# Expert biases by VectorE shuffles, and gathered rows in 1 KB pieces turned by VectorE, in a hybrid block with 32 experts

## The reference

```python
logits = u2 @ router_w + router_b
top_val, top_idx = lax.top_k(logits, 4)
gates = softmax(top_val)
# for each expert e, on the tokens that chose it:
hcat = xb @ w1[e] + b1[e]                  # 1024 -> 2048
h_glu, h_lin = split(hcat)
act = min(h_glu, 7) * sigmoid(1.702 * h_glu) * (clip(h_lin, -7, 7) + 1)
y = act @ w2[e] + b2[e]                    # 1024 -> 1024
# out = rms_norm(h + sum over the four of gate * y)
```

## Time and profile before

| | |
|---|---|
| median of three runs | 1619.48 us |
| span of the profiled execution | 1597.8 us |
| PE busy | 1571.5 us, 98% |
| VectorE (DVE) busy | 649.7 us, 41% |
| ScalarE (ACT) busy | 384.0 us, 24% |
| POOL busy | 444.7 us, 28% |
| moved by DMA | 493.10 MB, 309 GB/s over the span |

### The profile page before, as it was taken

One profiled execution on the slowest core, in us unless ns is written; L12 is line 12 of the kernel. 1 busy time (PEld: TensorE's weight loads), 2 busy tenths in 40 slices (PEclk: granted clock), 3 DMA queues, 4 the chain that ended last, 5 costly groups with the idle time before them and its releaser, 6 DMA issues.

```text
span 1597.8 us, 38945 instructions
## 1 busy us (share of the span) xinstructions
PE 1571.5 (98%) x16458; PEld 902.0 (56%) x16458; DVE 649.7 (41%) x1249; ACT 384.0 (24%) x601; POOL 444.7 (28%) x513
## 2 busy tenths in 40 slices
PE   7999999999999999999999999999999999999997
PEld 6998988877889644334433344334433443344334
DVE  4799898016242742224222332233222322232248
ACT  5333134346222311111111121122112111211112
POOL 7334333462433642111211111111211121112114
PEclk9999999999999999999999999999999999999999
DMA  7553242321275699999999999999999999999995
GB/s 217 159 179 112 79 144 95 90 72 51 79 294 224 204 340 406 407 416 414 412 398 410 412 409 398 414 407 408 394 411 407 410 392 404 411 412 400 403 413 236
DMA packets 129781, 493.10 MB, mean 309 GB/s; under 512 B 14379, under 2 KB 72099, under 8 KB 79973
## 3 DMA queue, kind: packets, MB, share of 16 engines
q1 hardware_dynamic: 110932, 464.61, 74.6%
q0 software_dynamic: 9168, 16.78, 3.2%
q10 hardware_dynamic: 9632, 11.03, 2.2%
HBM read 476.32 MB, written 24.87 MB: 314 GB/s over the span
## 4 chain that ended last, share of the span: by engine, by line
PE 95%; POOL 1%; ACT 1%; SPq 1%; DMA 1%; DVE 1%; issue 0%; POOLq 0%; DVEq 0%; ACTq 0%
PE banks L1619 41%; PE banks L1147 27%; PE banks L1668 21%; PE banks L1606 2%; DMA stage<-in_w_in_dram 1%; PE banks L1551 0%; PE banks L1639 0%; SPq L461 0%; PE banks L1506 0%; POOL h_res L787 0%; PE banks L1379 0%; POOL w_lo L624 0%; POOL w_lo L633 0%; POOL small L611 0%; SPq L447 0%
## 5 line engine op out<-in xcount | busy, mean ns | idle before, releaser
L1619 PE MATMUL banks<-w_ring,xT 128*32 128x512 f32 x6144 | 670.9, 592 | 0.1
L1619 PEld LDWEIGHTS banks<-w_ring,xT 128*32 128x32 f32 x6144 | 197.8, 110 | 431.3 <-issue 422.4
L1668 PE MATMUL banks<-w_ring,actT 128*32 128x256 f32 x6144 | 343.9, 380 | 0.0
L1668 PEld LDWEIGHTS banks<-w_ring,actT 128*32 128x32 f32 x6144 | 195.3, 110 | 144.8 <-issue 19.3
L2118 DVE TENSOR_TENSOR hid<-banks,bias 128x512 f32<-128x512 f32 x96 | 63.8, 665 | 475.6 <-PE banks L1619 475.6
L633 POOL TENSOR_TENSOR w_lo<-stage,w_hi 128x2048 fp32r<-128x2048 f32 x38 | 175.3, 4614 | 258.0 <-ACT w_hi L832 258.0
L1147 PE MATMUL banks<-u_hi,w_hi 128*128 128x264 f32 (+1 forms) x528 | 176.8, 335 | 1.5 <-POOL w_lo L624 1.5
L1147 PE MATMUL banks<-u_hi,w_lo 128*128 128x264 f32 (+1 forms) x528 | 175.1, 332 | 0.0
L1147 PE MATMUL banks<-u_lo,w_hi 128*128 128x264 f32 (+1 forms) x528 | 174.7, 331 | 0.0
L706 POOL COPY token_now<-token_of 96x1 int32 x32 | 6.6, 205 | 541.0 <-PE banks L1606 540.9
L1108 ACT ACTIVATE bias<-banks 128x512 f32<-128x512 f32 x32 | 19.1, 598 | 568.4 <-PE banks L1639 568.4
(11 more groups left out here) (311 smaller groups left out, 1586.7 us busy)
## 6 DMA issues: line engine op xcount, KB each, us to landing
w_ring<-in_expert_w_dram SPq DMA_DIRECT2D x384, 1024.0 KB, 17.6
stage<-in_w_in_dram SPq DMA_DIRECT2D x20, 1024.0 KB, 5.3
stage<-in_w_in_dram SPq DMA_DIRECT2D x16, 512.0 KB, 5.6
y_rows<-empty_row ACTq DMA_DIRECT2D x8, 1024.0 KB, 4.8
y_in<-y_rows SPq DMA_DIRECT2D x4, 2048.0 KB, 20.8
stage<-in_conv_pw_w_dram SPq DMA_DIRECT2D x4, 1024.0 KB, 5.2
stage<-in_mlstm_out_w_dram SPq DMA_DIRECT2D x4, 1024.0 KB, 5.2
stage<-in_w_out_dram SPq DMA_DIRECT2D x4, 1024.0 KB, 5.5
```

Source lines behind the costliest of these rows:

```text
L1619: last = nc.tensor.matmul(banks[32 * g:32 * (g + 1), t].rearrange("p (c j) -> p c j", j=64), xT[:, k, 32 * t:32 * (t + 1)], units, start=k ...
L1668: last = nc.tensor.matmul(banks[32 * g:32 * (g + 1), 3 + t, 0:GRP], actT[:, t, k], w2_ring[k // 2][:, k % 2, GRP * g:GRP * (g + 1)], start ...
```

## The change

Two parts.

*Biases.* They are loaded once in a layout in which partition 32g + e has the biases of expert e for the columns of group g (bias_turn, 128x768 float32, eight DMAs). For each expert a VectorE shuffle copies partition 0 of each block of 32 to all 32 (bias1, 512 columns; bias2, 256 columns), and another turns bias_turn by one partition in each block. The products on TensorE, the copies and the row pick on ScalarE, and the split on VectorE are gone.

*Rows.* u2 is written with its columns regrouped, so that a token's row in DRAM is four pieces of 1 KB. A gather is now three indirect DMAs (one for each group of 32 slots) of 128 pieces: piece g of a slot's token goes to partition 32g + slot. Slots are dealt over the 32 partitions of a block in steps of four (SPREAD = 8, TURNS = 4): slot s of a group stands in partition 4 * (s % 8) + s // 8. VectorE transposes the pieces in 32x32 blocks into xT. The slot tables are read back by 16 loads and converted on POOL in three rounds. w_router is loaded in eight DMAs, and last_g on POOL's queue.

```diff
-            sp.dma_start(w_router, router_w[0].rearrange("(k p) e -> p k e", p=P)).then_inc(router_in, 16)
+            for h in range(2):
+                for k in range(CG):
+                    sp.dma_start(w_router[32 * k:32 * (k + 1), h::2],
+                                 router_w[0].rearrange("(h k g j) e -> h k j g e", h=2, k=CG, g=CG)[h, k]).then_inc(router_in, 16)
...
-            sp.dma_start(last_g, final_norm_g.rearrange("(a d) -> a d", a=1).to_broadcast([P, D])).then_inc(row_bc_in, 16)
...
-                pool.indirect_dma_start(out=xs, out_offset=None, in_=u2_dram,
-                                        in_offset=bass.IndirectOffsetOnAxis(ap=token_now, axis=0),
-                                        bounds_check=last_token, oob_is_err=False).then_inc(xs_in, 16)
+                for t in range(TG):
+                    pool.indirect_dma_start(out=xs[:, t], out_offset=None, in_=u2_pieces,
+                                            in_offset=bass.IndirectOffsetOnAxis(ap=piece_now[:, t:t + 1], axis=0),
+                                            bounds_check=last_piece, oob_is_err=False).then_inc(xs_in, 16)
...
-            pool.dma_start(token_of[:, 0:PASSES * NE].rearrange("i (q e) -> i q e", e=NE),
-                           by_slot).then_inc(table_in, 16)
+            by_turn = table.rearrange("(x b a e) o -> b a x (e o)", b=TURNS, a=SPREAD, e=NE)
             for g in range(CG):
-                for t in range(TG):
-                    pool.dma_start(row_of[32 * g:32 * (g + 1), t, 0:PASSES * NE].rearrange("i (q e) -> i q e", e=NE),
-                                   by_slot[32 * t:32 * (t + 1)]).then_inc(rows_in, 16)
-            pool.wait_ge(table_in, 16)
-            chain(nc.gpsimd.tensor_scalar(token_part, token_of, -1.5, 0.25, ALU.add, ALU.mult))
-            chain(nc.gpsimd.tensor_scalar(token_part, token_part, TO_WHOLE, None, ALU.add))
-            chain(nc.gpsimd.tensor_scalar(token_of, token_part, -TO_WHOLE, None, ALU.add))
+                for b in range(TURNS):
+                    pool.dma_start(code_of[32 * g + b:32 * (g + 1):TURNS], by_turn[b]).then_inc(rows_in, 16)
+            pool.wait_ge(rows_in, 16 * CG * TURNS)
+            for t in range(TG):
+                codes = code_of[:, t::TG]
+                pieces = piece_of[:, t, 0:PASSES * NE].rearrange("p (q e) -> p q e", e=NE)
+                rows = row_of[:, t, 0:PASSES * NE].rearrange("p (q e) -> p q e", e=NE)
+                chain(nc.gpsimd.tensor_scalar(token_part, codes, -1.5, 0.25, ALU.add, ALU.mult))
+                chain(nc.gpsimd.tensor_scalar(token_part, token_part, TO_WHOLE, None, ALU.add))
+                chain(nc.gpsimd.tensor_scalar(token_part, token_part, -TO_WHOLE, None, ALU.add))
+                nc.gpsimd.tensor_scalar(pieces, token_part, float(CG), group_of, ALU.mult, ALU.add)
+                chain(nc.gpsimd.tensor_scalar(rows, codes, float(CG), group_of, ALU.mult, ALU.add))
+            pool.dma_start(last_g, final_norm_g.rearrange("(a d) -> a d", a=1).to_broadcast([P, D])).then_inc(last_g_in, 16)
...
-                    pool.wait_ge(xs_used, n + 2)
+                    pool.wait_ge(xT_made, (n + 2) * TG)
                     gather(n + 2, n * IDX + 4)
...
-                    act.wait_ge(bias_mm, n * 2 + 1)
-                    nc.scalar.activation(bias1, banks[:, 3].rearrange("p (h n) -> p h n", h=2), ACT.Copy).then_inc(bias_made, 1)
-                    act.wait_ge(bias_mm, n * 2 + 2)
-                    nc.scalar.activation(bias2, banks[:, 4, 0:GRP], ACT.Copy).then_inc(bias_made, 1)
-                    pick_rows(e + 1)
...
-                    act.wait_ge(xs_used, n + 2)
-                    for m in range(2):
-                        nc.scalar.activation(xT[:, 4 * m:4 * m + 4], banks[:, m, 0:4 * SLOTS].rearrange("p (k s) -> p k s", s=SLOTS),
-                                             ACT.Copy).then_inc(xT_made, 1)
...
-                        if k == KT - LATE - 1:
-
-                            for g in range(CG):
-                                last = nc.tensor.matmul(
-                                    banks[32 * g:32 * (g + 1), 3].rearrange("p (c j) -> p c j", j=64), row_pick,
-                                    bias_top[:, 0:2 * D].rearrange("p (c g j) -> p g c j", g=CG, j=64)[:, g],
-                                    start=True, stop=True, tile_position=(0, 32 * g))
-                            last.then_inc(bias_mm, 1)
...
-                    second(0)
-
-                    pe.wait_ge(actT_made, n * TG + 2)
-                    x_transposes(n + 1)
-                    second(1)
-                    second(2)
+                    for t in range(TG):
+                        second(t)
...
-                nc.vector.scalar_tensor_tensor(out=u2[:, i], in0=h_res[:, i], scalar=h_rstd[:, i:i + 1], in1=gf_bc,
-                                               op0=ALU.mult, op1=ALU.mult).then_inc(u2_made, 1)
+                for g in range(CG):
+                    nc.vector.scalar_tensor_tensor(out=u2[:, i, GRP * g:GRP * (g + 1)].rearrange("p (k j) -> p k j", j=32),
+                                                   in0=of_group(h_res[:, i], g), scalar=h_rstd[:, i:i + 1], in1=of_group(gf_bc, g),
+                                                   op0=ALU.mult, op1=ALU.mult).then_inc(u2_made, 1)
...
+            for t in range(TG):
+                dve.wait_ge(rows_mm, TG if t else 1)
+                nc.vector.transpose(xT[:, t].rearrange("p k s -> p (k s)"), first_xs(t)).then_inc(xT_made, 1)
...
                     assert k[0] == STEPS
-                    dve.wait_ge(bias_made, n * 3 + 3)
-
+                    dve.wait_ge(xs_in, (n + 1) * (16 * TG))
+                    for t in range(TG):
+                        nc.vector.transpose(xT[:, t].rearrange("p k s -> p (k s)"), xs[:, t]).then_inc(xT_made, 1)
+                    nc.vector.stream_shuffle(bias2, bias_turn[:, 2 * GRP:3 * GRP], [0] * NE).then_inc(bias2_made, 1)
                     dve.wait_ge(idx_step, n * IDX + 2)
                     for t in range(TG):
                         dve.wait_ge(y_mm, n * TG + (t + 1))
+                        if t == 0:
+                            dve.wait_ge(bias2_made, n + 1)
+                        elif t == 1:
+                            dve.wait_ge(bias_turned, n + 1)
                         nc.vector.tensor_tensor(y_out[:, t], banks[:, 3 + t, 0:GRP], bias2, ALU.add).then_inc(y_made, 1)
+                        if t == 0:
+                            nc.vector.stream_shuffle(bias_turn, bias_turn, [(r + 1) % NE for r in range(NE)]).then_inc(bias_turned, 1)
+                        elif t == 1:
+                            first_bias()
```

More of the change, by code:

```diff
@@ L79 @@
 PASSES = -(-SEQ // SLOTS)
-PARTS = 3
+SPREAD = 8
+TURNS = 32 // SPREAD
 NONE = 1 << 14
@@ L683, in _ @@
             nc.gpsimd.memset(carrier, 0.0)
-            nc.gpsimd.memset(token_of, NONE)
+            nc.gpsimd.memset(piece_of, NONE)
             nc.gpsimd.memset(row_of, NONE)
-            nc.gpsimd.memset(xs, 0.0)
-            for m in range(PARTS):
-                chain(nc.gpsimd.tensor_copy(expert_row[NE * m:NE * (m + 1), 0:NE], ident[NE * m:NE * (m + 1), NE * m:NE * (m + 1)]))
-            nc.gpsimd.tensor_copy(expert_row[:, NE:NE + 1], expert_row[:, 0:1]).then_inc(moe_consts, 1)
+            nc.gpsimd.memset(xs, 0.0).then_inc(moe_consts, 1)
             pool.wait_ge(moe_consts, 3)
@@ L792, in hybrid_block, with first_xs, of_group @@
         X_BANKS = (3, 0)
+        def first_xs(t):
+            return banks[:, X_BANKS[1 if t else 0], GRP * (t // 2):GRP * (t // 2 + 1)]
+        def of_group(rows, g):
+            return rows.rearrange("p (k g j) -> p g k j", g=CG, j=32)[:, g]
         def rows_copied(i, f):
@@ L1586, in _ @@
             places(1)
-            for m in range(2):
-                first_rows(0, m)
+            first_rows(0)
             places(2)
-            for m in range(2):
-                first_rows(1, m)
+            first_rows(1)
             places(3)
@@ L1594, in _ @@
             for i in range(2, TT):
-                for m in range(2):
-                    first_rows(i, m)
+                first_rows(i)
             pe.wait_ge(in_slot_made, 2 * TT)
@@ L1600, in _ @@
             last.then_inc(place_mm, 1)
-            def x_transposes(n):
-                pe.wait_ge(xs_in, n * 16)
-                for k in range(KT):
-                    last = nc.tensor.transpose(banks[:, k // 4, SLOTS * (k % 4):SLOTS * (k % 4 + 1)], xs[:, P * k:P * (k + 1)],
-                                               ident[0:SLOTS, 0:SLOTS])
-                last.then_inc(xs_used, 1)
             pe.wait_ge(passes_made, 1)
```

127 lines of the change are left out of this document (57 added, 70 removed).

## The result

The kernel before took 1620.49 us (median of four, 1618.56 to 1622.12), the changed one 1672.03 us (1671.65 to 1672.87). The ratio is 1.032, with a 95% interval of 1.031 to 1.034: 3.2% slower, where 1602.5 us had been forecast and the range ended at 1619.

A forecast was written before the change was run, and what follows sets the result against it. PE bounds the loop at 32.26 us per expert, DMA within 0.1 us; the bound passes to DMA. Span 1597.8 - 16.5 - 1.5 + 2.5 - 1.8 + 0.3 = 1580.8, plus 21.7: 1602.5 us; range 1588 to 1619.

The forecast's parts named there:

- the step on PE: Expert loop: the two layers' 384 matmul records stay as they are; PE's period goes from 32.26 to 31.11 us.
- the step on POOL: Expert loop: three gather DMAs add 2.7 us of POOL time per expert, hidden before the next index copy.
- Time against span: Whole run: the median of 1619.5 us lies 21.7 us above the profiled span, added to the forecast span.
- rival 1: Expert loop: PE stays the bound, E (DMA time beyond weights) 1.35 us or so; 1593.5 us; chance 0.22 with anything below.
- PE, -1.15 us per expert: Expert loop: bias products (0.23 + 0.11 us) and transposes (0.81 us) leave PE, 36.8 us over 32 experts.
- DMA, E from 2.3 to 1.75: Expert loop: DMA time per expert beyond 30.0 us of weights falls; period 31.75 us, gain 16.5 us, bound becomes DMA.
- lower end: Range of the forecast: 1588 us, from PE staying the bound with a stall of only 5 us (1588.5).
- Rival 3: Expert loop: the gather's four times as many pieces disturb the weights; E, DMA time beyond weights, 2.7; 1631 us; chance 0.10.
- VectorE: Expert loop: gains transposes (1.34 us) and three shuffles (2.7 us) per expert; hidden, 13 us busy per period.
- The start: Before the loop: first expert at 542 us; PE stalls once, about 9 us, for expert 2's rows; sum +2.5, tables -1.5.
- rival 4: Expert 2's stall: a 9 us pause could cost PE its 2.4 GHz for some microseconds, hidden while DMA binds; no chance given.
- The tail: After the loop: 1.8 us of slack gained, 0.3 us added for VectorE's new work there.

The follow-up runs named there:

- e10: The changed kernel, unaltered, on a chip where the kernel before took 1598.59 us; 1569.37 us, ratio 0.982.
- e8: The changed kernel without its gathers from expert 2 on (expert 1's rows used again); 1580.83 us, ratio 0.974 to the kernel before.
- e14: The changed kernel with its three gathers behind the expert's scatters, where the kernel before took 1620.23 us; 1575.39 us, ratio 0.973.
- e1: The kernel before with the biases' part alone, its old gather and PE's transposes kept; 1596.78 us, ratio 0.9987.
- e2: The rows' part alone, with the products for the biases kept as in the kernel before; 1581.76 us, ratio 0.990.
- e11: The rows' part alone, bias products kept, where the kernel before took 1598.59 us; 1582.45 us, ratio 0.990.
- e13: The kernel before, unaltered, traced on a chip where it is slower than in the profile shown; 1620.55 us.
- e15: The changed kernel with gathers behind the scatters, paced by PE's use of chunks 0, 2 and 4 of the next expert; 1579.96 us, ratio 0.976.
- e19: The rows' part alone, bias products kept, where the kernel before took 1598.90 us; 1582.44 us, ratio 0.989.
- e20: The changed kernel with two gathers in the old place and the third behind the scatters; 1573.16 us, ratio 0.984.

## Why the prediction was wrong, step by step

**PE beside POOL: the step that failed.** "The 384 matmul records of an expert's two layers stay as they are. PE's new period is 31.11 us", said the step on PE, and the step on POOL priced the three gathers in POOL's own time: "+2.7 us" per expert, "Hidden". What they do to PE was put at nothing, without a reason. In the runs that were forecast the records slow down beside the row of five indirect DMAs: 34.1 us per expert in place of 31.11, where 31.75 had been taken for the slower of PE and DMA. Against e10 that is 102.4 us of span (1670.4 - 1568.0). e8 and e14 take the row away, and the slow pieces go with it. No row of the trace that was read could show this, since e10, of that trace's kind, has five in a row beside the second layer without harm. How POOL's work slows PE, and why on one kind alone, stays open.

**Time against span.** "The median of the runs lies 21.7 us above that span" was taken as an offset; it was a difference of kind. This did not make the miss, because 1619.5 us was the right starting point for the second kind, where the runs were made. It hid that the rows read came from the other kind. There the sum had a span of 1580.8 us, rival 1 had 1572, and e10 has 1568.0: 29.8 us gained where 17.0 were summed up.

**PE, -1.15 us per expert.** Right, a little low: 32.26 - 30.96 = 1.30 (e10).

**DMA, E from 2.3 to 1.75.** The reading of before was right (e1 has 32.4 us where it waits for chunks), though "3.3 us lost in 14 experts" would have given 32.5 and not 32.3. The new value was mis-sized. e10's chunks, asked for from 640 to 700 us and from 1400 to 1462:

```profile
DMA to landing us min/median/max: 9.0/13.0/13.9
```
```profile
DMA to landing us min/median/max: 17.7/22.3/23.0
```

The median grows by 9.3 us in some 760 us, 0.38 us per expert, while PE takes 30.96. So the DMA needs about 31.3 us and E is about 1.3 (an estimate from these rows), rival 1's value. Its bytes say the same: POOL's queue moves 13.46 MB from 700 to 1500 us, 0.52 MB per period, with the chunks 13.10, and 419 x 30.96 = 12.97 MB are moved. e2, where PE itself takes 31.31 us, has a landing that hardly grows (10.4 and 11.3 us in the same windows). So the bound did go over to the DMA, as forecast, but a lead of landing time covers it: behind the stall and its slow start only the 29th to the 31st expert of e10 take longer than 30.96 us (31.19, 31.26 and 31.94). By this estimate a longer loop would run at the DMA's 31.3, and the biases' part would bring next to nothing there. (The prediction's lower end had a slip: with a stall of 5 us rival 1 comes to 1589.7 and not 1588.5.)

Gain of the rows' part alone: 16.1 us, of the biases' part alone 1.8, of the biases' part on top of the rows' 13.1 (e11 to e10): the new gather made the room that the other part needs, 1.0 us of the DMA per expert. The rule of the Trainium skill weighed for rival 1 ("DMA: Bandwidth & Descriptors", "The descriptor swizzle": fixed runs of four partitions for each engine) agrees with this, though the dealing by itself was not tried, and the section on back-pressure that the prediction put beside it is about transfers between cores, which no run here has.

**Rival 3, slower by the gather's pieces.** Right in its place and its sign, wrong in its mechanism and price. It let the descriptors disturb the weights and came to 1631 us at most. In the result PE never waits for a weight chunk in the loop, and the chunks' median landing is 10.1 us, as in the kernel before on that kind (10.4 in e13). Disturbed was PE itself. The count that mattered stood in the prediction's own step on POOL ("+2.7 us, hidden"): five indirect DMAs now follow one another beside the second layer. It was priced in POOL's time alone.

**VectorE.** The three shuffles take 0.44, 1.03 and 0.73 us, 2.2 in all, where 2.7 were taken, and the transposes 0.40 each. Busy time is 12.05 us per period, forecast 13. Hidden in the loop, as said.

**The start.** On the first kind the first expert starts at 541.17 (forecast 542), and expert 2 waits once, as forecast, but 3.0 us and not 9; the first layer behind it takes 22.3 us in place of 20.6, its first records at half pace (rival 4, the clock: granted 0.50, so 1.2 GHz, from 608 to 610 us, and 1.00 again from 612 on). From e10's timeline, and one of its windows:

```profile
606.34 19.07 PE L1601 MATMUL banks<-w_ring,xT 128*32 128x512 f32 x160 [3.04 <-DVE xT L2106]
```
```profile
608.00:610.00 2.00, 2.00 (x12) 0.45 (x8) 1.28 (x3) 0.00 (x0) 0.74 (x4) 0.50 1.03 434
```

POOL's conversions took 9.5 us in place of 8.8, but its table loads were all issued at 576.2 and not at 580.5, and the request went out at 595.6 and not at 601.8.

**The tail.** Forecast -1.8 + 0.3. In e10, 29.5 us lie between the end of PE's last second layer (1538.5) and the span's end, before 23.0 (1574.8 to 1597.8). So 6.5 us were lost here, and the 0.3 was the most mis-sized term of the sum on this kind of chip. PE's first products of the end now wait for VectorE, which has transposes and shuffles among its sums there:

```profile
1541.89 2.97 PE L1660 MATMUL banks<-y_out,selT 32*128 32x256 f32 x32 [2.10 <-DVE y_out L2115]
```

The account for the first kind: -0.9 (start) - 41.6 (32 x 1.30) + 4.7 (stall and half pace) + 6.5 (tail) = -31.3; measured 1568.0 - 1597.8 = -29.8. Most of the 1.5 between them are the longer 29th to 31st experts. For the second kind, against e13: -1.6 (start, 546.2 and 547.8) + 46.2 (the 32 experts, 1095.9 and 1049.7) + 5.5 (tail, 28.4 and 22.9) = 50.1; measured 1670.4 - 1620.4 = 50.0. That the second kind's stall at expert 2 is missing is no credit to the sum: the first expert, slowed to 39.0 us, hides it.

## What to carry to other kernels

Before a forecast is laid on a profile, hold its span against the times that it is meant to explain: a distance that differs from the 1.7 or 1.8 us of the other runs here says that profile and times come from different conditions, and it is no offset to add. An engine that is "hidden" is so in time only; count how many of its indirect DMAs now follow one another and what PE does beside them. Here one change of place, the gathers behind the scatters and so beside the first layer, gives 1575 us on the second kind (one chip) and 1573 us on the first (two chips, 3 us above the changed kernel as it stands there), and is the version to take: 2.7% and 1.6% under the kernel before, while the changed kernel as it stands is 3.2% over on the one and 1.8% under on the other.

## What was not expected of the hardware

The same program differs by 100 us between chips (1569.4 and 1672 to 1685 us), steadily within each. On the second kind PE's supply falls to about four records in 0.7 us while POOL makes a row of indirect DMAs. It is not PE's pace alone: in the result VectorE has a gap of 3.26 us between two transposes (541.56 to 545.26) beside a row of table writes. What it waits for there, PE's products of the first rows, ended at 540.8 by the trace, so the signal or VectorE was late too. On the first kind (e10) the three transposes stand together in 1.1 us.

```profile
541.56 0.44 DVE L2027 STREAM_TRANSPOSE xT<-banks 128x256 f32<-128x256 f32 x1
...
545.26 0.78 DVE L2027 STREAM_TRANSPOSE xT<-banks 128x256 f32<-128x256 f32 x2 [3.26 <-remote]
```

The load of chunk 8 shows the same. It waits for the 144th record of the second layer, which ends near 1024.8 in the chain of the result and near 1008.1 in e10's; SP's queue issues it 2.8 us later in the one (first line) and 0.2 us later in the other:

```profile
1027.67 3.60 SPq L490 DMA_DIRECT2D w_ring<-in_expert_w_dram  x4
```
```profile
1008.32 2.92 SPq L490 DMA_DIRECT2D w_ring<-in_expert_w_dram  x4
```

The Trainium skill ("Runtime: NRT & Kernel Launch", section "Instruction fetch mechanics") describes instructions that each engine loads by its own DMA queue in blocks of 16 KB, and says that a taken branch can stall on them. In the loop the trace shows no such loads: between 700 and 1500 us the changed kernel's DMA has packets of two queues only, the weights' and POOL's.

```profile
q1 hardware_dynamic: 40617, 295.81, 90.3%
q0 software_dynamic: 6624, 11.80, 4.2%
```

Outside this stretch the same trace does record such loads, 48 packets of two instruction queues. So the loads of that section are not what slows PE in the loop, as far as the trace shows them. What POOL's work and the other engines' issue share, and what sets the two kinds apart (the chip itself, or how a program is placed on it), was not found. The same kind held for all executions of a group. Two groups, e13 to e15 and e19 and e20, ran on chips listed under the same number and were of different kinds; whether that was one chip isn't known.
